# Seven z tiles of the state-space part computed between the attention's units and read back from DRAM

## The reference, cut to what matters

```
proj = rmsnorm(x) @ w_in
q, k, v, z, xbc, dt, ga, gb = split(proj, (1024, 256, 256, 2048, 3072, 32, 1024, 1024))
attn = stick_breaking_attention(norm(q), k_past + norm(k), v_past + v)
xs, B, C = split(silu(causal_conv(xbc)))           # 2048, 4*128, 4*128
y = ssd(xs, dt, A, B, C, state) + d_skip * xs      # 32 heads in 4 groups
y = group_rmsnorm(y * silu(z))                     # z gates y, 512 columns per group
x = x + (sigmoid(ga) * (attn @ w_pa) + sigmoid(gb) * (y @ w_pb)) @ w_out
x = x + (silu(h2 @ w_gate) * (h2 @ w_up)) @ w_down # h2 = rmsnorm(x), width 2816
```

## Time and profile before

| | us |
|---|---|
| three runs, median (lowest to highest) | 1595.26 (1593.65 to 1600.72) |
| the profiled execution's own time | 1595.28 |
| its span in the profile | 1593.8 |
| TensorE busy | 1487.8 |
| VectorE busy | 855.0 |
| ScalarE busy | 623.6 |
| GpSimd busy | 306.4 |

### The profile page before, as it was taken

The page is one execution under the profiler, slowest core; times in us unless marked ns, Lnnn a source line. Parts: engine busy times, 40 slices in busy tenths (PEclk is TensorE's granted clock), DMA queues, the critical chain, the costliest instruction groups (busy, mean ns, idle before and its releaser), DMA issues. The chain is left out here.

```text
span 1593.8 us, 27472 instructions
## 1 busy us (share of the span) xinstructions
PE 1487.8 (93%) x10851; PEld 1398.6 (88%) x10851; DVE 855.0 (54%) x1076; ACT 623.6 (39%) x1013; POOL 306.4 (19%) x406
## 2 busy tenths in 40 slices
PE   5998999887999999999999999988999999999997
PEld 4997778776899889889988988888999999999997
DVE  3454457888227666675666566546444444442221
ACT  4574456766124434532532344132242323332211
POOL 2011331000121543343143405421100000000000
PEclk9999999998899998999999999988999999999999
DMA  3244662111342232223222222336223223223331
GB/s 109 80 113 145 206 188 86 50 55 57 90 120 80 80 93 58 83 80 92 75 67 80 80 73 68 92 94 206 66 67 89 82 79 91 79 79 94 98 100 45
DMA packets 190262, 146.29 MB, mean 92 GB/s; under 512 B 8392, under 2 KB 178544, under 8 KB 190111
## 3 DMA queue, kind: packets, MB, share of 16 engines
q1 hardware_dynamic: 175394, 97.93, 21.2%
q0 software_dynamic: 14384, 46.62, 9.4%
q10 hardware_dynamic: 384, 0.37, 0.1%
HBM read 124.51 MB, written 20.39 MB: 91 GB/s over the span
## 5 line engine op out<-in xcount | busy, mean ns | idle before, releaser
L431 PE MATMUL tile_banks<-x_hi,w_hi 128*128 128x288 f32 (+1 forms) x1808 | 524.2, 305 | 13.6 <-ACT gate_out L1595 7.8
L432 PE MATMUL tile_banks<-x_lo,w_hi 128*128 128x288 f32 (+1 forms) x1808 | 511.9, 298 | 0.0
L435 PE MATMUL tile_banks<-x_hi,w_lo 128*128 128x288 f32 (+1 forms) x1808 | 390.1, 297 | 0.0
L431 PEld LDWEIGHTS tile_banks<-x_hi,w_hi 128*128 128x128 f32 (+1 forms) x1808 | 345.9, 191 | 19.9 <-issue 10.0
L432 PEld LDWEIGHTS tile_banks<-x_lo,w_hi 128*128 128x128 f32 (+1 forms) x1808 | 345.7, 191 | 1.8
L405 DVE TENSOR_TENSOR w_lo<-w_raw,w_hi 128x1024 fp32r<-128x1024 f32 (+2 forms) x169 | 220.5, 1305 | 177.7 <-ACT w_hi L399 176.8
L435 PEld LDWEIGHTS tile_banks<-x_hi,w_lo 128*128 128x128 f32 (+1 forms) x1808 | 294.6, 190 | 0.4
L399 ACT ACTIVATE w_hi<-w_raw 128x1024 fp32r<-128x1024 f32 (+2 forms) x169 | 175.5, 1039 | 103.0 <-PE tile_banks L435 102.1
L432 PE MATMUL tile_banks<-f_lo,w_hi 128*128 128x288 f32 x352 | 98.3, 295 | 0.0
L431 PE MATMUL tile_banks<-f_hi,w_hi 128*128 128x288 f32 x352 | 97.8, 294 | 0.0
L888 POOL DMA_DIRECT2D out_y_prompt<-y_tok x8 | 6.3, 787 | 410.5 <-ACT y_tok L1859 398.9
(11 more groups left out here) (340 smaller groups left out, 2645.3 us busy)
## 6 DMA issues: line engine op xcount, KB each, us to landing
w_raw<-in_w_in SPq DMA_DIRECT2D x68, 512.0 KB, 3.7
w_raw<-in_w_gate SPq DMA_DIRECT2D x22, 512.0 KB, 3.7
w_raw<-in_w_up SPq DMA_DIRECT2D x22, 512.0 KB, 3.7
k_page<-in_cache_k SPq DMA_DIRECT2D x64, 128.0 KB, 2.6
v_page<-in_cache_v POOLq DMA_DIRECT2D x64, 128.0 KB, 2.8
old<-in_state_ssm POOLq DMA_DIRECT2D x32, 256.0 KB, 3.3
out_ssm_sample<-old POOLq DMA_DIRECT2D x32, 256.0 KB, 2.8
w_raw<-in_w_pb SPq DMA_DIRECT2D x16, 512.0 KB, 3.3
```

The lines of the kernel that those rows point to most:

```text
L431: nc.tensor.matmul(out, wh, xh[:, HALVES[h]], start=start and k == 0, stop=False, skip_group_check=onto)
L432: nc.tensor.matmul(out, wh, xl[:, HALVES[h]], start=False, stop=False, skip_group_check=onto)
L435: mm = nc.tensor.matmul(out, wl, xh[:, HALVES[h]], start=False, stop=stop and k == last, skip_group_check=onto)
```

## The change

Seven z tiles, (0,0), (0,1), (0,2), (1,2), (1,3), (2,2) and (2,3), are no longer chunks of the state-space part. They are filler tiles 16 to 22. The filler slots of the prompt's steps hold 2 and 1 k-steps in place of 1 and 1, and those of the last three steps, which have no logits, 4 and 4. An early z tile is copied out of PSUM without its silu and goes to `gates_dram`; POOL's queue reads a group's two or three back into `z_s` at the group's start (`early_z_in`, for g > 0 when the group before has read its own), and ACT applies the silu in place at the end of step c = 2 (`early_z`). Of the remaining chunks, several that were listed second in their step are now listed first.

```diff
--- before.py
+++ after.py
@@ -133,11 +133,11 @@
 
     N_FIRST = KD + 2 + 2 + 1
     C_FILL = N_FIRST
-    N_FILL = 2 * KD
+    Z_EARLY = [(0, 0), (0, 1), (0, 2), (1, 2), (1, 3), (2, 2), (2, 3)]
+    N_FILL = 2 * KD + len(Z_EARLY)
     C_PA = C_FILL + N_FILL
     C_SSD = C_PA + KD
-    C_GROUP = 10 + 4
-    C_OUT = C_SSD + NG * C_GROUP
+    C_OUT = C_SSD + NG * (10 + 4) - len(Z_EARLY)
     C_FFN = C_OUT + KD
     C_DOWN = C_FFN + 2 * KF
     N_CHUNKS = C_DOWN + 3 * KD
@@ -147,8 +147,7 @@
     assert T_FILL % 2 == 1
     T_PA = T_FILL + 2 * N_FILL - 1
     T_SSD = T_PA + KD
-    T_GROUP = 10 + KD
-    T_OUT = T_SSD + NG * T_GROUP
+    T_OUT = T_SSD + NG * (10 + KD) - len(Z_EARLY)
     T_FFN = T_OUT + KD
     T_DOWN = T_FFN + 2 * KF
 
@@ -452,27 +451,27 @@
 
 
 
-            z = [("z", g, j) for j in range(PG)]
+            z = {j: ("z", g, j) for j in range(PG)}
             pb = [("pb", g - 1, n) for n in range(0, KD, 2)]
             into = group_inputs(g + 1)
             if g == 0:
-                return [([z[1]], [into[0]]), ([z[2]], [into[1]]), ([z[3]], [into[2]]), ([], [into[3]]), ([into[4]], [into[5]]),
+                return [([z[3]], [into[0]]), ([into[1]], []), ([into[2]], []), ([into[3]], []), ([into[4]], [into[5]]),
                         ([("z", 1, 0)], [("z", 1, 1)])]
             if g < NG - 1:
-                return [([z[2]], [into[0]]), ([z[3]], [pb[0]]), ([into[1]], [pb[1]]), ([into[2]], [pb[2]]), ([into[3], into[4]], [into[5]]),
+                return [([into[0]], []), ([into[1]], [pb[0]]), ([into[2]], [pb[1]]), ([into[3]], [pb[2]]), ([into[4]], [into[5]]),
                         ([pb[3]], [("z", g + 1, 0), ("z", g + 1, 1)])]
             return [([z[2]], []), ([z[3]], [pb[0]]), ([], [pb[1]]), ([], [pb[2]]), ([], []), ([pb[3]], [])]
 
         last_pb = [("pb", NG - 1, n) for n in range(0, KD, 2)]
 
-        before_groups = group_inputs(0) + [("z", 0, 0)]
+        before_groups = group_inputs(0)
         ssd_chunks = before_groups + [key for g in range(NG) for pair in ssd_plan(g) for keys_ in pair for key in keys_] + last_pb
         chunk_of = {key: C_SSD + n for n, key in enumerate(ssd_chunks)}
         tile_of, n_t = {}, T_SSD
         for key in ssd_chunks:
             tile_of[key] = n_t
             n_t += 2 if key[0] == "pb" else 1
-        assert n_t == T_OUT and len(ssd_chunks) == NG * C_GROUP
+        assert n_t == T_OUT and len(ssd_chunks) == C_OUT - C_SSD
 
         def ssd_col(key):
             what, g, j = key
@@ -514,7 +513,7 @@
         STEPS_A = NU + 3
         caps = []
         for t in range(STEPS_A):
-            caps += [2, 2] if t < FIRST_PROMPT else [1, 1]
+            caps += [2, 2] if t < FIRST_PROMPT else [2, 1] if t < NU else [4, 4]
         filler = filler_steps(N_FILL, KD, caps)
         tile_end = {}
         for n, todo in enumerate(filler[:-1]):
@@ -614,7 +613,11 @@
             def fill_src(n):
 
                 if n < N_FILL:
-                    col = COL_GA + n * P if n < KD else COL_GB + (n - KD) * P
+                    if n < 2 * KD:
+                        col = COL_GA + n * P if n < KD else COL_GB + (n - KD) * P
+                    else:
+                        g, j = Z_EARLY[n - 2 * KD]
+                        col = COL_Z + (g * PG + j) * P
                     return w_in[0, :, col:col + P].rearrange("(t p) n -> p t n", p=P)
                 n -= N_FILL
                 return w_pa[0, :, n * P:(n + 1) * P].rearrange("(t p) n -> p t n", p=P)
@@ -790,6 +793,14 @@
                 eng.tensor_copy(conv_out[:, ct, 3:27].rearrange("p (b t) -> p b t", b=NB), seqs[:, :, TD:TD + 3]).then_inc(sem("conv_tails"), 1)
                 eng.wait_ge(sem("conv_tails"), n + 1)
 
+            def early_z_in(g):
+
+                if g:
+                    eng.wait_ge(sem("y_gated"), PG * g)
+                for j in range(PG):
+                    if (g, j) in Z_EARLY:
+                        eng.dma_start(z_s[:, j, :], gates_dram[2 * KD + Z_EARLY.index((g, j))]).then_inc(sem("early_z_in"), 16)
+
             def old_states_in(g, b):
 
                 n = g * NB + b
@@ -818,6 +829,7 @@
                 conv_io(key)
             for g in range(NG):
 
+                early_z_in(g)
                 eng.wait_ge(sem("b_tok_made"), g + 1)
                 if g:
                     wait_full(eng, ("new_state", g - 1, NB - 1))
@@ -1592,7 +1604,7 @@
                 wait_tile(eng, t)
                 if f >= 2:
                     eng.wait_ge(sem(f"gate_stored{f % 2}"), 16 * (f // 2))
-                eng.activation(halves(gate_out[:, f % 2, :]), tile(t), ACT.Sigmoid).then_inc(tile_free[t % 2], 1)
+                eng.activation(halves(gate_out[:, f % 2, :]), tile(t), ACT.Sigmoid if f < 2 * KD else ACT.Copy).then_inc(tile_free[t % 2], 1)
                 make_hi(C_FILL + f + 2, after_tiles=t + 1)
 
             def copy_outputs(part):
@@ -1747,6 +1759,13 @@
                     eng.activation(e_t[:, :, 0:m], spare(key).rearrange("p (j l) -> p j l", l=P)[:, :, 0:m], ACT.Exp)\
                        .then_inc(bank_read[use[key][0]], 1)
 
+            def early_z(g):
+
+                for j in range(PG):
+                    if (g, j) in Z_EARLY:
+                        eng.wait_ge(sem("early_z_in"), 16 * sum(k <= g for k, _ in Z_EARLY))
+                        eng.activation(z_s[:, j, :], z_s[:, j, :], ACT.Silu).then_inc(sem("early_z_made"), 1)
+
             def sequence(g, b):
                 key = ("old_t", g, b)
                 wait_full(eng, key)
@@ -1769,6 +1788,8 @@
                         sequence(g, b)
                     for key in later:
                         slot(key)
+                    if c == 2:
+                        early_z(g)
                 before, later = plan[5]
                 flush()
                 eng.wait_ge(sem("conv_done"), 6 * min(g + 2, NG))
@@ -2084,7 +2105,7 @@
                 wait_tile(eng, t)
                 eng.wait_ge(sem(f"ga_back{n % 2}"), 16 * (n // 2 + 1))
                 if n < 2:
-                    eng.wait_ge(sem(f"gate_stored{n % 2}"), 16 * (N_FILL // 2))
+                    eng.wait_ge(sem(f"gate_stored{n}"), 16 * ((N_FILL + 1 - n) // 2))
                 else:
                     eng.wait_ge(sem(f"gated_out{n % 2}"), 16 * (n // 2))
                 eng.tensor_tensor(halves(gate_out[:, n % 2, :]), tile(t), halves(ga_in[:, n % 2, :]), ALU.mult).then_inc(tile_free[t % 2], 1)
@@ -2255,7 +2276,10 @@
                 eng.wait_ge(sem("y_added"), NC * (g + 1))
                 wait_after_read(eng, ("y_new", g, 0))
                 for j in range(PG):
-                    wait_freed(eng, tile_of[("z", g, j)])
+                    if (g, j) in Z_EARLY:
+                        eng.wait_ge(sem("early_z_made"), Z_EARLY.index((g, j)) + 1)
+                    else:
+                        wait_freed(eng, tile_of[("z", g, j)])
                     eng.tensor_tensor(y_t[:, j, :], y_t[:, j, :], z_s[:, j, :], ALU.mult).then_inc(sem("y_gated"), 1)
                 before, later = plan[5]
                 for key in before:
```

## The result

The changed kernel takes 1626.62 us (median of four executions, 1623.79 to 1630.75) against 1595.3 (four, 1593.65 to 1600.72): ratio 1.019, 95% interval 1.0154 to 1.0226, so **some 30 us slower**. The forecast was 1590. The profiled execution is 1626.73 us long, its span 1625.2.

What follows compares the result with a forecast made beforehand. TensorE, busy 1487.8 of 1593.8 us, was taken as the bound, with DVE pacing the attention. 1595.3 + 14.3 (attention) - 19.2 (state-space part) = 1590.4 us, with an 8-in-10 range of 1575 to 1605.

Steps and rivals of the forecast that it cites:

- Attention, pairs: Prompt's attention: seven added tiles make TensorE the bound; a pair of heads grows from 18.5 to 20.1 us, +11.5 in all.
- the turn-round: Fillers' single PSUM area in the attention: TensorE waits for ACT to copy the last tile out, 1.4 us a pair.
- the end: End of the attention, last product with v through the first `w_pa` tile: 30.1 us for 27.3, +2.8.
- Rival 2: Attention: waiting for the fillers' PSUM area decides, 2.1 us a tile, 22.2 us a pair, 1606 us in all; chance 0.16.
- The fillers fit: Attention: added k-steps fit TensorE's slack, DVE keeps the pace at 18.9 us a pair, 1582 us in all; chance 0.17.
- c = 4: State-space groups 1 and 2: this step loses one of three tiles, others still cover its chain; gains 2 x 6.3 = 12.6 us.
- c = 1: State-space groups 1 and 2: two tiles stay, but the convolution comes ahead of the outputs; +2.2 us, twice.
- More gaps bring more of the lower clock: State-space part: one further half-rate stretch costs TensorE at most some 2.6 us; 1.7 taken off the gain.
- The chain POOL, DVE, TensorE: State-space one-tile steps: this chain replaces the removed tile as what sets the length, 20.8 to 22.1 us in group 0.
- z(0,0): Tile ahead of the state-space groups: removing it gains only 1.0 us (0 to 1.4); the rest turns into waiting.
- 4 had steps that don't shrink: State-space part: no steps shrink except the two three-tile ones, gain 8.2 us, 1601 us in all; chance 0.10.
- slower: Whole kernel: the outcome of being slower by over 0.5% (8 us), given a chance of 0.21.

Runs made afterwards that it cites:

- the copies first: The changed kernel with ACT copying a finished filler tile out before it reads the weights, for tiles ending ahead of the transposes: 1613.89 us, 1.0098 to the kernel before.
- the attention's part alone: The kernel before plus seven z tiles computed and stored in the attention, never read; the state-space part still computes all twelve: 1615.44 us, ratio 1.0123.

## Why the prediction was wrong

The profiled executions are 31.4 us apart, where 4.9 less was forecast. By place, measured and forecast: to the first `w_pa` tile +24.3 (+14.3), from there to the groups -1.2 (-1.0), the groups +2.6 (-18.2), behind them +5.8 (nothing). The second profile of the changed kernel has -6.6 in the groups.

- **Attention, pairs: right in kind, short in size.** TensorE became the bound and waits only at the area. "A pair becomes 20.1 us": 20.65. Its own work, seen with the copies first, is 19.4 (forecast 18.7), and the turn-round is the rest, 1.25 (forecast 1.4). From logits to logits +15.6 for +11.5. The rest of the missing sum: 1.2 us in the units ahead, 1.8 between the last logits and the product with v, and the end, +5.7 less 0.8 of regained clock, for +2.8, which had taken all 2.3 us at 1.2 GHz as regained. In all +24 for **+14.3**. Rival 2 named this wait; it reached 0.97 us a tile, not 2.1. The forecast's 0.82 was a mean over nine tiles of which only four ended ahead of the transposes.
- **"The fillers fit" was rightly refused.** With next to no wait left TensorE is at its bound, and its weight loads are busy for 116.48 of 128 us (window above): by the rule of the Trainium skill (Perfetto Trace Analysis, Identifying the Most-Contended Engine), which judges headroom by that share, it would have 9% to spare. The trace of this case does not agree; the starts judged it rightly.
- **c = 4: right** (-12.7 for -12.6), c = 1 too (+3.8 for +4.4). That c = 4 agrees to 0.1 us is luck: with the attention's part alone the same three-tile steps took 51.04 us each for 54.12 and 54.41.
- **"More gaps bring more of the lower clock ... I take 1.7 off": the step that failed.** It priced the clock as one further stretch; it falls in each of the five one-tile steps (0.75 to 0.82). The mean clock over the groups went from 0.93 to 0.89. The work lost is at most one minus the clock times the length, since TensorE also waits at the lower clock: 0.07 x 520.4 = 36 before, 0.11 x 523.0 = 58 after, 21 us more. The forecast for this stretch was -18.2, measured +2.6, a difference of 21. The second profile (0.91, 513.85 us) gives 10 and 12. With clocks of two digits the estimate is good to some 5 us, so the closeness of the first pair is luck. The chain POOL, DVE, TensorE was not priced too short (20.7 us at full clock where 22.1 was forecast). The clock took its gain away. c = 2 of group 0 took 26.8 us for 22.1: 3.6 of the excess are slow sequences behind the wait (7.6 us for 4.0), 1.1 the later state (19.2 us into the step for 18.0), behind slow segments and a slow tile at the step's head.
- **z(0,0): right.** 5.0 of its 6.3 us turned into waiting; from the first `w_pa` tile to the groups it is -1.2 for -1.0.
- **The first step: luck.** Group 0's c = 0 gave 5.0 us that no term had. It took 20.6 to 21.5 us in twelve of the fifteen profiles here, and 25.3 to 25.6 in three, before's among them, in which TensorE waits some 3 us for DVE's `xend` (3.1 in before's). It goes with no edit of this step; why it comes is open.
- Behind the groups the same instructions took 562.5 us for 556.7. Of the profiles here only one more, the one whose groups end at the same time as before's, has 556.9; the others have 558.9 to 565.5, whether that part begins earlier or later. I have no experiment on it: its cause is open.
- None of the four rivals is what happened: 2 named the attention's wait, at twice its size; 4 had steps that don't shrink, though not that they grow, and by another cause. The forecast gave "slower" 0.21.

## What to carry to other kernels

A tile that covers a chain was worth more here than its length: it also kept TensorE's clock up. Before taking work out of a stage with narrow matmuls, price what stays at half rate from that stage's own slow rows, once per repetition, not once per stage. Take tiles from the step that has the most of them and no more than the other stage's slack holds (two here gained 0.2 to 0.4%, where seven lost 1.9%), and then put behind the outputs whatever delays the engine that TensorE will wait for (1.0% gained with two, 0.3% with seven and ACT's copy first).

## What was not expected of the hardware

- The clock fell with TensorE busy for 23.87 of 24.27 us: behind 0.33 us of waiting, among products of 8 and 128 columns; wide matmuls between them stopped it, in one profile, in c = 2 and 3 of group 0.
- It falls at the same place of each step once steps are alike (26.83 us at 0.88, several in a row), and the same instructions took 504 or 520 us by when the stage began. Executions of one kernel differed by 22 us (0.966 and 0.952). Four executions of a kernel left intervals of 0.4 to 0.7% either side, ten to twelve of 0.2 to 0.4%.
